# A hybrid RWKV-7 and differential-attention encoder on one core: load depths, stage borders and the split of a solve changed

## What is computed

```python
u = rmsnorm(h, norm_pre);  proj = u @ w_in                      # 1024 x 4288
c = centred_conv(proj[:, :1728], rw_conv_w, rw_conv_b)          # r, k, v and the low-rank inputs, 3 taps
y_rw = rwkv7_mixer(c, ...) * silu(proj[:, 1728:2240])           # both directions, 8 heads of 64
#   per head, per token: S = S * w + (S a) b^T + v k^T;  y = S r
q, k, v = proj[:, 2240:3776]                                    # 4 heads, 2 maps of 64, values of 128
y_da = diff_attention(q, k, v, ...) * silu(proj[:, 3776:])      # softmax1 - lam * softmax2, ALiBi distances
h = h + concat(y_rw, y_da) @ w_out
out = h + sigmoid(h @ ple_gate_w + ple_gate_b) * rmsnorm(p @ ple_proj, ple_norm)
```

## Time and profile before

| what | us |
|---|---|
| median of 3 runs | 3906.74 (3905.64 to 3915.66) |
| profiled execution | 3906.6, its span 3904.6, mean granted clock 0.965 |
| conv: to its last TensorE column / next stage begins | 653.7 / 696.6 |
| projection: TensorE from / to / next stage begins | 711.2 / 1417.1 / 1467.2 |
| units: TensorE from / chain stage begins | 1474.2 / 2329.1 |
| chain: next stage begins | 2421.9 |
| attention: next stage begins | 3187.9 |
| output: end of span | 3904.6 |

### The profile page before, as it was taken

How to read it: one execution, slowest core, us unless ns; L and a number is a source line. 1 busy time by engine, 2 the same in 40 slices (tenths; PEclk the granted TensorE clock), 3 DMA queues, 4 the chain that set the end, 5 groups by cost and what they waited for, 6 DMA issues and landing times. The chain is left out here.

```text
span 3904.6 us, 56389 instructions
## 1 busy us (share of the span) xinstructions
PE 3519.7 (90%) x21081; PEld 2317.1 (59%) x21081; DVE 2418.1 (62%) x4280; ACT 1402.6 (36%) x2571; POOL 409.1 (10%) x682
## 2 busy tenths in 40 slices
PE   7999997799999957888888876799999968999998
PEld 6788776344444426777777765367666644444444
DVE  3566656699999954555555544677777744444443
ACT  3444444132322312222222220566666642222232
POOL 0243334000000002211121110000000000000000
PEclk9999998899999978999999998899999989999999
DMA  4343434523223213333333334300000032222221
GB/s 143 130 146 109 135 119 130 192 86 113 86 81 113 94 74 106 120 103 101 92 95 98 93 104 154 110 14 11 13 13 13 11 128 88 69 74 77 77 77 42
DMA packets 307943, 355.03 MB, mean 91 GB/s; under 512 B 122380, under 2 KB 234712, under 8 KB 305312
## 3 DMA queue, kind: packets, MB, share of 16 engines
q1 hardware_dynamic: 294304, 341.82, 26.6%
q10 hardware_dynamic: 13440, 10.49, 0.9%
HBM read 194.95 MB, written 157.29 MB: 90 GB/s over the span
## 5 line engine op out<-in xcount | busy, mean ns | idle before, releaser
L906 PE MATMUL rs_tm<-rs_w,rs_uT 128*128 128x512 f32 x1600 | 692.6, 594 | 25.0 <-DMA rs_w<-in_w_in_dram 25.0
L906 PEld LDWEIGHTS rs_tm<-rs_w,rs_uT 128*128 128x128 f32 x1600 | 303.4, 191 | 400.6 <-issue 399.0
L561 PE MATMUL cv_pj<-cv_uT,cv_w 128*128 128x257 f32 (+1 forms) x2240 | 503.7, 382 | 0.8 <-DVEq L420 0.8
L561 PEld LDWEIGHTS cv_pj<-cv_uT,cv_w 128*128 128x128 f32 (+1 forms) x2240 | 410.7, 186 | 90.3 <-issue 22.9
L1545 PE MATMUL at_g<-at_kT,at_qz 64*128 64x512 f32 x1088 | 303.2, 632 | 29.1 <-DMA at_kT<-scratch_q_kT 24.3
L834 DVE TENSOR_TENSOR rs_tmp<-rs_tt,rs_al 128x63 f32<-128x63 f32 (+31 forms) x315 | 284.1, 902 | 23.6 <-DMA rs_al<-scratch_ablk 14.2
L836 DVE TENSOR_TENSOR rs_tt<-rs_tt,rs_tmp 128x63 f32<-128x63 f32 (+31 forms) x315 | 288.8, 917 | 10.8
L1568 PEld LDWEIGHTS at_pb<-at_v,at_attT 128*128 128x128 f32 x2176 | 249.8, 192 | 64.5 <-issue 47.0
L1497 DVE CUSTOM_DVE_ANT_0 at_sca<-at_g,at_nd 128x1024 f32<-128x1024 f32 (+1 forms) x144 | 167.8, 1165 | 181.0 <-PE at_g L1545 181.0
L1813 PE MATMUL fn_gb<-fn_wg,fn_hT 128*128 128x512 f32 x640 | 278.0, 592 | 1.7 <-ACT fn_hT L1673 1.7
L1813 PE MATMUL fn_hb<-fn_wo,fn_mixT 128*128 128x512 f32 x640 | 278.8, 594 | 0.3 <-ACT fn_mixT L1673 0.3
(11 more groups left out here) (243 smaller groups left out, 5352.8 us busy)
## 6 DMA issues: line engine op xcount, KB each, us to landing
un_pk<-scratch_packs SPq DMA_DIRECT2D x80, 640.0 KB, 4.0
scratch_packs<-cv_pk SPq DMA_DIRECT2D x20, 2048.0 KB, 6.7
cv_x<-in_x_dram SPq DMA_DIRECT2D x20, 512.0 KB, 3.5
scratch_uT<-cv_uT SPq DMA_DIRECT2D x5, 2048.0 KB, 7.9
scratch_ablk<-cv_ab SPq DMA_DIRECT2D x80, 128.0 KB, 2.3
rs_uT<-scratch_uT SPq DMA_DIRECT2D x10, 1024.0 KB, 7.2
rs_w<-in_w_in_dram SPq DMA_DIRECT2D x5, 2048.0 KB, 19.3
rs_al<-scratch_ablk SPq DMA_DIRECT2D x5, 2048.0 KB, 11.2
```

The lines of the kernel that those rows point to most:

```text
L561: last = nc.tensor.matmul(pj[n % 3][0:r, 0:HALF], w[:, c, m * P:m * P + r], uT[b % 2][:, c, HALF * hf:HALF * hf + HALF], start=(c == 0), s ...
L906: last = nc.tensor.matmul(tm[n % 4][:, :], uT[b % 2][:, k, half], w[:, k, 512 * u:512 * u + 512], start=(k == 0), stop=(k == KC - 1))
```

## The change

- **conv.** `am` has two banks, `xb` is gone: the x transposes share bank `st` and wait for `packed` and `xt_evac`. `corners(k)` forms both halves of the rows in one block, half by half in turns. The last unit's products go to the spare `uT` buffer, not to `pk`, so they don't wait for a store, and VectorE forms four of the eight. While the tail runs, SP loads the first two weight blocks of the projection into the place of the convolution weights and the first window of uT into the place of the x tiles.
- **projection.** Uses these places; `rs_al` is its first load, then three weight blocks. The 5 x 63 solve steps are cut by cost into 54 pieces, 3 for each of the first 18 tiles; a finished group is turned by ScalarE at the start of the next tile and stored then.
- **units.** `pk`, `tt`, `tf` have three buffers, load n+3 follows unit n.
- **chain.** `ch_cb` has four buffers; `ysum` is loaded three steps ahead, not all at once.
- **output.** ident first; `ple_norm` and `gate_b` are loaded behind `wp`, VectorE waits for them later (`late_rows`).

```diff
+        spare = uT[NB % 2][:, :, :].rearrange("p k t -> p (k t)")[:, 0:NQ * PK_V].rearrange("p (q n) -> p q n", q=NQ)
+        def pk_of(k):
+            return spare if k == NK - 1 else pk
...
+            sp.wait_ge(s["pj_ready"], 28 * NB)
+            sp.dma_start(w[:, :, 0:512], w_v[:, :, REST_COLS[0]:REST_COLS[0] + 512]).then_inc(s["w_rest"], 16)
+            sp.wait_ge(s["xt_ready"], E + 2 * NT)
+            sp.wait_ge(s["u_stored"], 16 * (NB - 1))
+            sp.dma_start(x_pair[:, :].rearrange("p (k t) -> p k t", k=KC), uT_d[0][:, :, 0:2 * P]).then_inc(s["u_rest"], 16)
             for k in range(NK - 3, NK):
                 store_corners(k)
                 if k + 1 < NK:
                     store_pack(k + 1)
+                if k == NK - 3:
+                    sp.dma_start(w[:, :, 512:1024], w_v[:, :, REST_COLS[1]:REST_COLS[1] + 512]).then_inc(s["w_rest"], 16)
...
             for k in range(NK):
                 pool.wait_ge(s["exp_done"], 3 * k + 3)
                 pool.wait_ge(s["packed"], k + 1)
-                if k:
+                if k == NK - 1:
+                    pool.wait_ge(s["pj_ready"], 28 * (NB - 1))
+                    pool.wait_ge(s["u_stored"], 16 * (NB - 1))
+                elif k:
                     pool.wait_ge(s["pk_stored"], 48 * k)
-                    pool.wait_ge(s["am_ready"], 2 * k)
+                    pool.wait_ge(s["am_ready"], k)
+                products(nc.gpsimd, k, 0, "prod")
+                if k < NK - 1:
+                    products(nc.gpsimd, k, 1, "prod")
...
+            products(nc.vector, NK - 1, 1, "prod_last")
...
                 pe.wait_ge(s["xt_evac"], n)
+                if c == 4:
+                    pe.wait_ge(s["table_ready"], 1)
+                elif c > 4:
+                    pe.wait_ge(s["packed"], c - 4)
...
                     for q in range(NQ):
                         for i in range(2):
-                            at = 64 * (NQ * d + q)
-                            last = nc.tensor.matmul(am[64 * i:64 * i + 64, at:at + 64], pk[hs, q, rows_at + 64 * i:rows_at + 64 * i + 64],
-                                                    pk[hs, q, cols_at + 64 * i:cols_at + 64 * i + 64], start=True, stop=True)
+                            for h in range(2):
+                                hs = slice(64 * h, 64 * h + 64)
+                                at = 64 * (NQ * d + q)
+                                last = nc.tensor.matmul(am[h][64 * i:64 * i + 64, at:at + 64], own[hs, q, rows_at + 64 * i:rows_at + 64 * i + 64],
+                                                        own[hs, q, cols_at + 64 * i:cols_at + 64 * i + 64], start=True, stop=True)
...
+        steps = [(j, k) for j in range(NJ) for k in range(B - 1)]
+        total, pieces, done = sum(cost(k) for _, k in steps), [[] for _ in range(3 * NT - 6)], 0
+        for j, k in steps:
+            pieces[done * (3 * NT - 6) // total].append((j, k))
+            done += cost(k)
+        ended = {j: i // 3 for i, piece in enumerate(pieces) for j, k in piece if k == B - 2}
+        finished = {t: j for j, t in ended.items()}
...
-                slice_of(t, 0)
-                slice_of(t, 1)
+                solve(3 * t)
+                solve(3 * t + 1)
                 qk_sums(t)
-                slice_of(t, 2)
+                solve(3 * t + 2)
                 gate(t, 3)
-            j = NJ - 1
-            nc.vector.tensor_copy(al[j % 2][:, :, :], tt[j % 2][:, :, :].rearrange("p j t -> p t j")).then_inc(s["turned_last"], 1)
             gate(NT - 1, 4)
...
-            load(0, 0)
-            load(1, 1)
+            for n in range(3):
+                load(n)
             for n in range(NI - 2):
                 sp.wait_ge(s["wz_ready"], n + 1)
                 sp.wait_ge(s["ad_ready"], n * 4 + 4)
                 sp.sem_inc(s["passed"], 1)
-                load(n + 2, n % 2)
+                if n + 3 < NI:
+                    load(n + 3)
                 store(n, n % 2)
...
-                if t >= 2:
-                    sp.wait_ge(s["y_evac"], 2 * t - 2)
+                if t >= 4:
+                    sp.wait_ge(s["y_evac"], 2 * t - 6)
...
+            for step in steps[0:3]:
+                local_in(step)
             for i, first, t, chunk, last in steps:
+                if t + 3 < NCH:
+                    act.wait_ge(s["h_ready"], t + 1)
+                    local_in(steps[t + 3])
...
-            for dst, src, n in ((ln_g, ln_g_d, 512), (ln_b, ln_b_d, 512), (ple_norm, ple_norm_d, D_MODEL), (gate_b, gate_b_d, D_MODEL)):
-                sp.dma_start(dst[:, :], src.broadcast_to([P, n])).then_inc(s["rows"], 16)
+            for dst, src in ((ln_g, ln_g_d), (ln_b, ln_b_d)):
+                sp.dma_start(dst[:, :], src.broadcast_to([P, 512])).then_inc(s["rows"], 16)
             sp.dma_start(wo[:, :, :], w_v[0]).then_inc(s["wo"], 16)
             sp.dma_start(wp[:, :, :], w_v[2]).then_inc(s["wp"], 16)
+            for dst, src in ((ple_norm, ple_norm_d), (gate_b, gate_b_d)):
+                sp.dma_start(dst[:, :], src.broadcast_to([P, D_MODEL])).then_inc(s["late_rows"], 16)
             sp.dma_start(wg[:, :, :], w_v[1]).then_inc(s["wg"], 16)
```

More of the change, by code:

```diff
@@ L24 @@
 SLOPES = [2.0 ** (-8.0 * (h + 1) / DA_HEADS) for h in range(DA_HEADS)]
+REST_COLS = [CONV_COLS + at for at in (512, 1024, 1536, 0, 2048)]
 class Phase:
@@ L381, in _ @@
                     corner(k - 2, 0)
+                    corner(k - 2, 1)
                 if 1 <= k <= NK:
@@ L637, in _ @@
                 if k >= 2:
-                    corners(k - 2, 0)
+                    corners(k - 2)
                 if k < NK:
@@ L687, in rest_phase, with cost @@
         t_v, n_v = (t.rearrange("(g b q) (d l) e -> d b g q l e", g=G, q=4, d=2) for t in (tblk, nblk))
-        costs = [m * (max(n, 17) if n >= SHORT else 2 * n) + 160 for m, n in ((k + 1, B - 1 - k) for k in range(B - 1))]
-        ends = [0]
-        for i in range(12):
-            k, goal = ends[-1], sum(costs) * (i + 1) / 12
-            while k < B - 1 and sum(costs[0:k + 1]) <= goal + 0.5 * costs[k]:
-                k += 1
-            ends.append(k)
-        ends[12] = B - 1
+        def cost(k):
+            m, n = k + 1, B - 1 - k
+            return 160 + m * (max(n, 17) if n >= SHORT else 2 * n)
+        steps = [(j, k) for j in range(NJ) for k in range(B - 1)]
[5 more added lines that the diff above has]
+        finished = {t: j for j, t in ended.items()}
+        assert len(finished) == NJ
         @block.sync
@@ L815, in _, with solve @@
             st = Steps(dve, s["step"], 0)
-            def slice_of(t, i):
-                j, at = t // 4, 3 * (t % 4) + i
-                T, A = tt[j % 2], al[j % 2]
-                if at == 0:
-                    dve.wait_ge(s["cleared"], 2 * j + 2)
-                    dve.wait_ge(s[f"al_in{j % 2}"], 16 * (j // 2) + 16)
-                for k in range(ends[at], ends[at + 1]):
+            def solve(i):
+                for j, k in pieces[i] if i < len(pieces) else []:
+                    T, A = tt[j % 2], al[j % 2]
+                    if k == 0:
+                        dve.wait_ge(s["cleared"], 2 * j + 2)
+                        dve.wait_ge(s[f"al_in{j % 2}"], 16 * (j // 2) + 16)
                     m, n = k + 1, B - 1 - k
@@ L905, in _ @@
                     for k in range(KC):
-                        last = nc.tensor.matmul(tm[n % 4][:, :], uT[b % 2][:, k, half], w[:, k, 512 * u:512 * u + 512], start=(k == 0), stop=(k == KC - 1))
+                        last = nc.tensor.matmul(tm[n % 4][:, :], uT[b % 2][:, k, half], w[:, k, at:at + 512], start=(k == 0), stop=(k == KC - 1))
                     last.then_inc(s["tm_ready"], 1)
@@ L1002, in _ @@
         def _(pool):
+            for i in range(3):
+                nc.gpsimd.memset(tt[i][:, :, :], 0.0).then_inc(s["setup"], 1)
             for i in range(2):
-                nc.gpsimd.memset(tt[i][:, :, :], 0.0).then_inc(s["setup"], 1)
                 nc.gpsimd.memset(vz[i][:, :], 0.0).then_inc(s["setup"], 1)
-            n = 4
+            n = 5
             def setup(ins):
@@ L1245, in chain_phase @@
     with Phase(nc, "ch") as ph:
-        cb = [ph.sb(f"cb{i}", [P, 2, 256]) for i in range(2)]
+        cb = [ph.sb(f"cb{i}", [P, 2, 256]) for i in range(4)]
         ysum = ph.sb("ysum", [P, NCH, G * P])
@@ L1266, in _, with local_in @@
             for i, first, t, chunk, last in steps:
-                if t >= 2:
-                    sp.wait_ge(s["y_evac"], 2 * t - 2)
+                if t >= 4:
+                    sp.wait_ge(s["y_evac"], 2 * t - 6)
                 for d in range(2):
-                    sp.dma_start(cb[t % 2][:, d, :], carry_v[chunk[d]][d]).then_inc(s[f"carry{t % 2}"], 16)
+                    sp.dma_start(cb[t % 4][:, d, :], carry_v[chunk[d]][d]).then_inc(s[f"carry{t % 4}"], 16)
         @block.scalar
         def _(act):
-            for i, first, t, chunk, last in steps:
+            def local_in(step):
```

(1 more changed line is left out.)

181 lines of the change are left out of this document (97 added, 84 removed).

## The result

| | before | after |
|---|---|---|
| median | 3907.3 us (3905.6 to 3915.7, 4 runs) | 3741.8 us (3737.3 to 3748.6, 4 runs) |
| profiled span, granted clock | 3904.6 us, 0.965 | 3743.0 us, 0.975 |

The account below looks back on a forecast made before the run. It took TensorE to bound conv and projection (VectorE just behind), TensorE's load waits to cost units and chain, and stage borders to stand idle. Terms -34 - 65 - 25 - 1 = -125 from 3906.6 gave 3781 us, range 3742 to 3822.

Parts of the forecast that it names:

- The conv loop: Conv stage: one corner block of 32 products in place of two of 16, about 0.1 us a unit: -2 us (0 to -3).
- four at a time: Rival, conv loop: the corner products do run four at a time, 19 us less, 3762; chance 8%.
- the rule that it leaned on: Conv loop, Trainium skill: a weight load overlaps running matmuls only when its row group differs.
- The conv tail: End of conv stage: unit 19's products in spare room, split over GpSimd and VectorE: -7.5 us (-3 to -12).
- The port rule: Conv tail: two-input VectorE and GpSimd instructions block each other; the four pairs take about 1 us more than 6.4.
- The byte sum: Conv tail: 3 MB take 11.6 us, so 2.6 MB of packs and 2 MB of weights last to about 678.
- The projection: Projection stage: earlier start, solve in 18 tiles, stores issued beside work; -24.6 us, or -34 with conv included.
- the one that can turn: Projection, solve over 18 tiles: VectorE becomes the bound at 36.9 us a tile; the packing costs 23 us.
- The units: Unit stage: loads three deep remove TensorE's load waits, period floor 9.46 us: -65 us (-40 to -90).
- the term for the clock: Unit stage: about 25 us for stretches at half clock, taken to stay; their going counted only in the upper end, -90.
- Chain: Chain stage: carry loads four deep cut TensorE's waits for `ch_cb`: -25 us (-12 to -30).
- output: Output stage: VectorE and `fn_hb` start some 4 us sooner, but tile 1's transposes still wait for loads: -1 us (0 to -4).

Follow-up runs that it names:

- 19-tile kernel: The changed kernel with the solve cut into 57 pieces over 19 tiles in place of 54 over 18: 3731.2 us.

## Why the prediction was right or wrong

**The conv loop was wrong (-2 taken, -21 measured).** The failing step is the comparison in the earlier trace rows. It took the chain's `ch_hb` products as a pattern of halves by turns and saw the old pace in them. But each `ch_hb` product of row half h also writes column half h: two quarters, as many as the old corner blocks used, only other ones. The new order uses four. The prediction counted alternations where it should have counted different quarters. A second term was mis-sized: one block less to enter and leave was put at 0.1 us a unit, and the runs show 0.4. The rival that had this outcome was given 8%. Its name, four at a time, was right, and the rule that it leaned on was not (the row half alone does nothing). It said 19 us on top of the forecast's 2, just the 21 measured, and that is luck in part: the turns gave 13 us and the single block 8.

**The conv tail was half right (-7.5 taken, -4.1).** The side-by-side products were sized well: four pairs took 6.5 us (650.67 to 657.16), 1.6 us a pair, and 6.4 were said. The port rule of the Trainium skill that the prediction names there (SBUF — State Buffer, Who interferes with whom) would make it four times the lone times, 1.18 on GpSimd and some 0.67 on VectorE, 7.4 us. The engines do hinder each other (1.63 us a product on GpSimd and 1.67 on VectorE), but less than that. The failing step is the place of the loads in SyncE's queue. The prediction looked at the copies of the last unit only. But ScalarE's copy of unit 18's corners already waited for the stores of unit 17, which stood behind 3 MB of loads, and the exponentials for unit 19's products stood behind that copy: the products began 18.0 us after the last column, 15.7 said, and 13.5 once the order was changed. In the same way the last copies began 28.8 us after it, 25.2 said, behind the stores of unit 18's corners, and from there to the next stage it was 9.9 us, nine to ten said. That is the whole miss of 3.4 us. The byte sum held 3 MB and then 4.6 MB from 661 on; the tail as a whole moved 12. The last corner block was over-priced (3.9 us at half clock, 2.0 measured, the same error as in the loop), which changed nothing, as its copies waited for the stores.

**The projection was right**, and it was the part called the one that can turn. The start: TensorE 4.6 us into the stage (5.1 said), VectorE 10.9 (10.7). The solve: 682.19 to the end of tile 17's gates, 664.7 us in 18 tiles as computed. TensorE from its start to its last product 728.7 us, forecast 728.8. It waited for gates nine times, not once a tile, first at 906, in the seventh tile: it may run ahead by two units, and that took up the tiles before. The end: 10.6 us from the last product to the next stage, 12 said. The 19-tile kernel shows the cause itself.

**The units were undersized (-65 taken, -86), inside their bounds of -40 to -90.** The floor was right, 9.46 said and 9.41 found. The waits were about right, 66 said and 61 left over when the long units are taken out. The failing step is the term for the clock, put at nothing in the sum: the stretches at half clock were set aside as some 25 us that stay, and counted only into the upper end of the range. They came behind the waits that the change removed, and went with them: 24 us by the long units, 17 by TensorE's busy time.

**Chain (-25 and -28) and output (-1 and +0.6) were right**, in the output stage with the reason told: `fn_hb` started 3 us sooner and tile 1's transposes did not.

**The sum.** The two large misses have the same sign, so they didn't cancel. The range was made of the bounds of the parts and three rivals one at a time; it had no room for the corners together with the units' upper end, which is what came.

## What to carry to other kernels

- With products of 64 x 64, count how many different quarters of the array successive ones use, rows and columns. Two kinds of two-quarter orders ran alike here, four quarters made the steady pace double. Each switch into and out of such a block has its price too, here some 0.4 us for one block less.
- A wait of TensorE of a microsecond in ten costs more than itself where the granted clock falls now and then (here 17 to 24 us beside some 61): price the half-clock stretches with the wait that makes them.
- Spare DMA time in a stage's tail is soon full. Count the bytes of a tail before loads are moved into it, and look at which copies, and what behind them in the same engine's queue, wait for stores that queue behind those loads.

## What the runs showed of the hardware

- One or two row halves made no difference to 64 x 64 products: 1.91 us for 64 records in either order, 1.16 with four quarters by turns.
- With waits of TensorE (the first aside) of 1.35 us on average and 2.5 at most in a period of 10.5 us, the granted clock fell to its lower level seven times for 3.4 us. A 448-column product put ahead of each wait kept it at 1.00 for 822 us, and the stage was 10 us shorter although TensorE was busy 49 us more in it (781.6 in place of 732.5).
- Side by side, 128 x 512 float32 products of two tiles took 1.63 us on GpSimd and 1.67 on VectorE, in place of 1.18 and 0.67 alone.
- While sixteen stores of 256 KB, each from 16 partitions, were under way, 118 to 135 GB/s moved, with the DMA engines busy 0.32 to 0.35: 118 and 135 from one queue, 132 from two.
